# A decoder layer with a top-2 mixture of experts: routing on the unnormalized rows, whole-row gathers, a column-halved output product, slots dealt over the partitions

## What is computed

```python
y = jnp.concatenate([rmsnorm(yi, og[i]) for i, yi in enumerate((y_pool, y_rg, y_nsa, y_sc))], axis=-1)
x = x + jnp.einsum('blm,md->bld', y, lw['w_out'])
x = x + moe_ffn(rmsnorm(x, lw['norm_ffn_g']), lw['router_group_w'], lw['router_group_b'],
                lw['router_expert_w'], lw['router_expert_b'], lw['exp_w_gu'], lw['exp_w_down'])

def moe_ffn(x, wg_r, bg_r, we_r, be_r, w_gu, w_down):   # xt: the 520 rows
    lg = xt @ wg_r + bg_r                        # 4 groups, the best one is taken
    pg = softmax(lg);  gsel = argmax(lg)
    le = (xt @ we_r + be_r).reshape(T, 4, 8)     # 8 experts in each group
    tv, ti = top_k(le[gsel], 2)
    gate = pg[gsel] * softmax(tv)
    # for each of a token's two experts e:  a, b = split(x @ w_gu[e]);  y += gate * ((silu(a) * b) @ w_down[e])
```

## Time and profile before

| what | value |
|---|---|
| time, median of 3 runs (lowest, highest) | 896.74 us (896.69, 897.82) |
| the profiled execution's own time | 897.07 us |
| its span, first to last instruction | 895.3 us |
| granted TensorE clock, mean over the span | 0.962 of full speed |
| PE busy | 745.3 us (83%) |
| DVE, ACT, POOL busy | 217.6, 137.9, 186.9 us (24%, 15%, 21%) |
| moved by the DMA engines | 247.55 MB, 276 GB/s over the span |
| chain that ended last, by engine | PE 39%, SP's queue 33%, DVE 11%, DMA 11% |

### The profile page before, as it was taken

One profiled execution on the slowest core, in us unless ns is written; L12 is line 12 of the kernel. 1 busy time (PEld: TensorE's weight loads), 2 busy tenths in 40 slices (PEclk: granted clock), 3 DMA queues, 4 the chain that ended last, 5 costly groups with the idle time before them and its releaser, 6 DMA issues.

```text
span 895.3 us, 10055 instructions
## 1 busy us (share of the span) xinstructions
PE 745.3 (83%) x3636; PEld 384.8 (43%) x3636; DVE 217.6 (24%) x546; ACT 137.9 (15%) x338; POOL 186.9 (21%) x186
## 2 busy tenths in 40 slices
PE   3999999979898999829999997777777777787783
PEld 3788688857666545613333332222222222222220
DVE  4331104267759322171011110010010010100110
ACT  4212313013253401100000000000000000000000
POOL 6010000150300000011322331322312313223121
PEclk9999999989897999859999999999999999999997
DMA  9642823010510294458999999999999999999981
GB/s 309 127 135 60 262 103 102 4 69 1 207 77 1 83 423 181 164 225 339 413 410 408 408 406 415 415 408 417 409 412 414 410 413 416 408 416 409 413 341 30
DMA packets 75812, 247.55 MB, mean 276 GB/s; under 512 B 24796, under 2 KB 44139, under 8 KB 51163
## 3 DMA queue, kind: packets, MB, share of 16 engines
q1 hardware_dynamic: 62625, 232.00, 65.5%
q0 software_dynamic: 11776, 8.58, 4.4%
q10 hardware_dynamic: 1378, 6.54, 1.8%
HBM read 240.99 MB, written 24.92 MB: 297 GB/s over the span
## 4 chain that ended last, share of the span: by engine, by line
PE 39%; SPq 33%; DVE 11%; DMA 11%; issue 3%; ACT 2%; POOL 0%; ACTq 0%; DVEq 0%; POOLq 0%
PE bank L1063 36%; SPq L570 23%; SPq L577 9%; DMA reg_b<-in_exp_w_gu 6%; PE bank L1066 3%; DMA reg_a<-in_exp_w_gu 3%; DMA reg_x<-in_x_prompt 1%; DVE reg_a L1722 1%; DVE reg_a L1802 1%; DVE reg_y L1973 1%; DVE reg_a L1712 1%; DVE reg_x L1712 0%; DVE small L1763 0%; POOL small L673 0%; DVE reg_a L1714 0%
## 5 line engine op out<-in xcount | busy, mean ns | idle before, releaser
L1063 PE MATMUL bank<-reg_w,reg_y 128*64 128x512 f32 (+2 forms) x512 | 136.9, 585 | 19.3 <-DMA reg_w<-in_exp_w_gu 19.3
L1063 PE MATMUL bank<-reg_b,reg_y 128*64 128x512 f32 x528 | 124.3, 601 | 25.8 <-DMA reg_b<-in_exp_w_gu 18.0
L1063 PE MATMUL bank<-reg_a,reg_y 128*64 128x512 f32 x528 | 124.5, 607 | 24.0 <-DMA reg_a<-in_exp_w_gu 17.8
L1977 DVE TENSOR_TENSOR reg_y<-reg_y,bank 128x256 f32<-128x256 f32 x32 | 13.5, 421 | 426.5 <-ACT reg_y L1046 426.5
L1063 PEld LDWEIGHTS bank<-reg_w,reg_y 128*64 128x64 f32 (+2 forms) x512 | 46.1, 146 | 104.5 <-issue 59.6
L1063 PE MATMUL bank<-reg_b,reg_w 128*128 128x260 f32 x384 | 85.3, 383 | 0.0
L1063 PEld LDWEIGHTS bank<-reg_b,reg_y 128*64 128x64 f32 x528 | 34.1, 136 | 106.8 <-issue 56.5
L1063 PEld LDWEIGHTS bank<-reg_a,reg_y 128*64 128x64 f32 x528 | 34.5, 138 | 105.3 <-issue 50.6
L1063 PEld LDWEIGHTS bank<-reg_b,reg_w 128*128 128x128 f32 x384 | 72.7, 190 | 12.0 <-issue 1.1
L673 POOL TENSOR_TENSOR small<-small 128x1 f32<-128x1 f32 (+4 forms) x18 | 20.2, 1125 | 198.1 <-DVE small L1855 68.1
L739 POOL DMA_INDIRECT out_y_p<-reg_y,reg_q x16 | 25.3, 1581 | 170.6 <-ACT reg_y L1050 170.6
(11 more groups left out here) (341 smaller groups left out, 656.9 us busy)
## 6 DMA issues: line engine op xcount, KB each, us to landing
reg_a<-in_exp_w_gu SPq DMA_DIRECT2D x44, 1024.0 KB, 28.1
reg_b<-in_exp_w_gu SPq DMA_DIRECT2D x44, 1024.0 KB, 28.3
reg_w<-in_exp_w_gu SPq DMA_DIRECT2D x40, 1024.0 KB, 28.2
reg_a<-in_exp_w_down SPq DMA_DIRECT2D x22, 1024.0 KB, 28.5
reg_b<-in_exp_w_down SPq DMA_DIRECT2D x22, 1024.0 KB, 28.6
reg_h<-in_exp_w_down SPq DMA_DIRECT2D x20, 1024.0 KB, 28.8
reg_w<-in_w_in SPq DMA_DIRECT2D x9, 1024.0 KB, 10.7
reg_w<-in_w_out SPq DMA_DIRECT2D x1, 4096.0 KB, 13.2
```

The source lines that it names most:

```text
L1063: return eng.matmul(out, lhsT, rhs, start=start, stop=stop, skip_group_check=True)
L1977: tt(hid[b], silu[b], bank[2 + b][:, 256:512], ALU.mult).then_inc(S["hid_made"], 1)
```

## The change

Four things are changed together.

1. **The router reads the raw residual.** The gain is multiplied into the router's weights once (POOL, `rtw_scaled`), and the root is applied to the router's result, one number per token (`group_choice`). `second_norm` and the reordered `h2` are gone: PE turns `x1` itself (`turn_x1`).
2. **Whole raw rows are gathered.** `ffn_in` now holds `x1`. A gather takes 64 partitions of 4 KB. PE turns them with 8 transposes of 64 partitions at a column stride of 8, `copy_xe` multiplies by the gain, the root goes through its own three bf16 pieces to the slots (`gate_table` has 192 columns) and is applied in the silu's scale; the gate of a slot carries the other root.
3. **The output product goes by column halves.** PE makes the left halves of all tiles, then the right halves, with transposes and routing matmuls between their chunks. DVE chooses experts in two groups: tiles 4, 0, 1 early, tiles 2, 3 late. SP issues expert 2's down parts after the last transposes of the mixers, and its gate and up parts after Y3.0 and Y3.1.
4. **Slots are dealt over the partitions.** `cap_iota` gives slot 4a+b the rank a+16b, where it gave slot s the rank s.

The diff, cut:

```diff
-            eng.iota(cap_iota, pattern=[[0, 2], [1, CAP]], base=0, ...)
+            eng.iota(cap_iota, pattern=[[0, 2], [1, 16], [16, 4]], base=0, ...)
...
+            eng.tensor_tensor(rt_w, rt_w, params[:, P_FFN_G:P_FFN_G + 8].unsqueeze(2).to_broadcast([128, KC, 36]), ALU.mult).then_inc(S["rtw_scaled"], 1)
...
             def gather(e):
-                idx = bass.IndirectOffsetOnAxis(ap=row_of[:, e:e + 1], axis=0)
-                eng.indirect_dma_start(xe_rows[e % 2], None, h2_halves, idx, bounds_check=2 * T - 1, oob_is_err=False).then_inc(x_gathered[e % 2], 16)
+                at = slice(CAP * (e % 2), CAP * (e % 2) + CAP)
+                idx = bass.IndirectOffsetOnAxis(ap=row_of[0:CAP, e:e + 1], axis=0)
+                eng.indirect_dma_start(xe_rows[at], None, x1_dram, idx, bounds_check=T - 1, oob_is_err=False).then_inc(x_gathered[e % 2], 16)
...
# PE
-            for n in range(NTILE):
-                project_out(n)
-                if n:
-                    turn_h2(n - 1)
-            route(3)
-            turn_h2(4)
-            route(4)
+            for n in range(1, NTILE):
+                drained(eng, f"NT{TILES[n]}")
+                project_out(n, 0, {6: (turn_x1, (0, 0)), 7: (turn_x1, (0, 1))} if n == 1 else {3: (route, (0,))} if n == 2 else {})
+            project_out(1, 1, {4: (turn_x1, (1, 0))})
+            for n in range(2, NTILE):
+                project_out(n, 1, {2: (turn_x1, (n - 1, 1)), 5: (route, (n - 1,)), 7: (turn_x1, (n, 0))})
...
+            eng.wait_ge(S["mask_made"], 1)
+            positions("posA", range(3))
+            turn_x1(4, 1)
+            route(4)
+            eng.wait_ge(S["mask_made"], 2)
+            positions("posB", [3, 4])
...
-                    ins = mm(bank[0][:, 64:160], in_slot[:, m_, :], ids[:, m_ // 5, m_ % 5, 2:5]..., m_ == 0, m_ == 9)
+                    ins = mm(bank[0][:, 64:256], in_slot[:, m_ // 2, m_ % 2, :], scale_ids[:, m_ // 2, m_ % 2]..., m_ == 0, m_ == 9)
...
-                for j in range(4):
-                    ins = turn(bank[1][:, 128 * j:128 * j + 128], xe_rows[b][:, 128 * j:128 * j + 128])
+                by_channel = xe_rows[at, :].rearrange("n (p c) -> n c p", c=KC)
+                for c in range(KC):
+                    ins = eng.transpose(bank[1][:, CAP * c:CAP * c + CAP], by_channel[:, c, :], ident[at, at])
...
# DVE
-                second_norm(n)
+            drained(eng, "Y4.0")
+            tt(x1[0:NS, 4, :], x1[0:NS, 4, :], y_smp, ALU.add).then_inc(S["x1_smp"], 1)
+            ask_rstd(0)
+            for n in range(1, NTILE):
+                add_half(n, 0)
+            for n in range(1, 3):
+                add_half(n, 1)
+                ask_rstd(n)
+            early, late = range(3), range(3, 5)
+            group_choice(early)
+            add_half(3, 1)
+            expert_choice(early)
+            ask_rstd(3)
+            add_half(4, 1)
+            count_before(early, "posA")
+            ask_rstd(4)
+            find_slots(pk, early)
+            group_choice(late)
+            expert_choice(late)
+            count_before(late, "posB")
...
+            link(tt(gate, gate, rstd[:, 0:5].unsqueeze(2).to_broadcast([128, 5, 2]), ALU.mult))
+            for which in range(2):
                 for k in range(2):
-                    ins = eng.tensor_copy(ids[:, k, :, 2 + piece], ohp[:, k])
+                    factor = gate[:, :, k] if which == 0 else rstd[:, 0:5]
+                    ins = tt(ohp[:, :, k, :], oh[:, :, k, :], factor.unsqueeze(2).to_broadcast([128, 5, N_EXP]), ALU.mult)
+                link(ins)
+                for piece in range(3):
+                    out = scale_ids[:, :, :, 3 * which + piece, :]
+                    ins = eng.tensor_copy(out, ohp)
...
+                    if piece < 2:
+                        link(tt(ohp, ohp, out, ALU.subtract))
...
-                eng.tensor_copy(xe[b], bank[1][:, :].rearrange("p (j s n) -> p j s n", j=4, s=2)).then_inc(S["xe_made"], 1)
+                tt(xe[b], bank[1][:, :].rearrange("p (c n) -> p c n", c=KC), gain_x.unsqueeze(2).to_broadcast([128, KC, CAP]), ALU.mult).then_inc(S["xe_made"], 1)
...
# SP
-            eng.wait_ge(bank_full[bank_of["Y3.1"]], turn_of["Y3.1"] + 1)
-            load_gu(2, 2)
-            eng.wait_ge(S["h2_stored"], 16 * NTILE)
-            eng.wait_ge(bank_full[bank_of["hTb3"]], turn_of["hTb3"] + 1)
-            load_down(2, 2)
+            eng.wait_ge(bank_full[bank_of["NT3"]], turn_of["NT3"] + 1)
+            load_down(2, 2)
+            eng.wait_ge(bank_full[bank_of["Y3.0"]], turn_of["Y3.0"] + 1)
+            load_gu(2, 2, parts=(0, 1))
+            eng.wait_ge(bank_full[bank_of["Y3.1"]], turn_of["Y3.1"] + 1)
+            load_gu(2, 2, parts=(2, 3))
```

More of the change, by code:

```diff
@@ L153, in psum_jobs @@
         take(f"NT{i}")
-    last = None
     take("L", 7)
-    for i in TILES:
-        take(f"Y{i}.0")
-        if i < 4:
-            take(f"Y{i}.1")
-        if last is not None:
-            take(f"hTa{last}")
-            take(f"hTb{last}")
-        last = i
-    take("hTa3")
-    take("hTb3")
-    take("pos")
+    first, *others = TILES
+    take(f"Y{first}.0")
+    take(f"Y{others[0]}.0")
+    take(f"hTa{first}")
+    take(f"hTb{first}")
+    for i in others[1:]:
+        take(f"Y{i}.0")
+    take(f"Y{others[0]}.1")
+    take(f"hTa{others[0]}")
+    for last, i in zip(others, others[1:]):
+        take(f"Y{i}.1")
+        take(f"hTb{last}")
+        take(f"hTa{i}")
+    take("posA")
+    take(f"hTb{others[-1]}")
+    take("posB")
     take("cnt", 6)
@@ L351, in layer_kernel @@
         thr = small.cut(8)
-        valid = small.cut(5)
+        valid = small.cut(1)
         minus_half = small.cut(160)
@@ L561, in _, with load_gu @@
             eng.dma_start(x1[:, 0:4, :], x_dram).then_inc(S["x_reloaded"], 16)
-            def load_gu(e, g, free=None):
+            def load_gu(e, g, free=None, parts=range(GU_PARTS)):
                 width = KC // GU_PARTS
-                for part in range(GU_PARTS):
+                for part in parts:
                     lo = part * width
@@ L994, in _, with square, x1_turned @@
             eng.dma_start(o["rgh_s"].rearrange("l b c -> (l b) c"), tail_rows[16:24, 768:1024]).then_inc(S["tails_stored"], 16)
-            def sums(n):
+            def square(n, half):
                 i = TILES[n]
                 r = ROWS[i]
-                if i < 4:
-                    drained(eng, f"Y{i}.1")
-                else:
-                    ps = taken(eng, "Y4.0")
-                    for w in range(4):
-                        ins = copy(y_smp[:, 256 * w:256 * w + 256], ps[32 * w:32 * w + NS, 0:256])
-                    copied(ins, "Y4.0")
-                    eng.wait_ge(S["x1_smp"], 1)
-                eng.activation(h2[0:r, i, :], x1[0:r, i, :], ACT.Square, accum_out=sumsq[0:r, i:i + 1]).then_inc(S["x1_ss"], 1)
-            def h2_turned(n):
+                at = slice(512 * half, 512 * half + 512)
+                earlier = 5 + n if half and n else n + (n > 0) + half
+                if earlier >= 2:
+                    eng.wait_ge(S["x1_ss"], earlier - 1)
+                scratch = squares[0:r, 512 * (earlier % 2):512 * (earlier % 2) + 512]
+                eng.activation(scratch, x1[0:r, i, at], ACT.Square, scale=1.0 / 32, accum_out=x1_sq[0:r, n, half:half + 1]).then_inc(S["x1_ss"], 1)
+            def x1_turned(n, k):
                 i = TILES[n]
@@ L1907, in _, with add_half @@
[L1907 to L1913 removed]
+            def add_half(n, half):
+                i = TILES[n]
+                at = slice(512 * half, 512 * half + 512)
+                ps = taken(eng, f"Y{i}.{half}")
+                copied(tt(x1[:, i, at], x1[:, i, at], ps[:, :], ALU.add), f"Y{i}.{half}")
@@ new lines, in count_before, with find_slots @@
+            def count_before(g, job):
+                at = slice(g[0], g[-1] + 1)
+                ps = taken(eng, job)
+                cols = ps[:, 32 * g[0]:32 * g[-1] + 32].rearrange("p (t e) -> p t e", t=len(g))
+                for k in range(2):
+                    ins = tt(ohp[:, at, k, :], oh[:, at, k, :], cols, ALU.mult)
+                copied(ins, job)
+                drained(eng, job)
+                link(eng.tensor_reduce(pk[:, at, :], ohp[:, at], X_AXIS, ALU.add))
+            def find_slots(at, g):
+                lo, m_ = g[0], len(g)
+                tt(in_slot[:, lo:lo + m_].rearrange("p t k s -> p (t k) s"), cap_iota.unsqueeze(1).to_broadcast([128, 2 * m_, 2 * CAP]),
+                   at[:, lo:lo + m_].rearrange("p t k -> p (t k)").unsqueeze(2).to_broadcast([128, 2 * m_, 2 * CAP]), ALU.is_equal).then_inc(S["in_slot_made"], 1)
```

398 lines of the change are left out of this document (199 added, 199 removed).

## The result

The changed kernel takes **908.67 us** (median of 4 runs, 907.26 to 909.59) against 897.28 us before (4 runs, 896.69 to 897.98): ratio 1.0125, 95% interval 1.0106 to 1.0144. It is 11.4 us slower, where 884.6 us and a gain were predicted. The profiled execution took 909.55 us, its span is 907.7 us.

What follows compares the result with a forecast made beforehand. From expert 3 on only the weight transfers were taken to set the pace. Start -5.4 and finish -6.7 us summed to -12.1 on the profiled 897.07, giving 885.0, or 884.6 at the median; range 880.5 to 892.5.

Steps and rivals of the forecast that it cites:

- The bytes don't change: a row of 4 KB is gathered once where two halves were: Gathers beside the expert weights: same bytes in whole rows, only where the rows sit changes; no cost to the stream counted.
- The middle of the experts still at 1.02 and 410 GB/s: Sign that the forecast is right: mid-expert DMA share and rate stay as in the kernel before.
- Bound by the stream from expert 3 on: Experts from about 400 us: only weight transfers set the pace; PE is busy 82 of 100 us.
- Start, 5.4 us: Chain before the first freed-buffer weight issue: SP issues at 399.5 instead of 404.94, bounds 3 to 8 us.
- DVE's late choice: Expert choice after the last tile's routing: DVE starts at 377.8, 3.7 us sooner; mask at 381.35.
- pieces: bf16 splitting of gate and root on DVE after the indices: 7.3 us instead of 4.8, done at 393.7.
- The new last wait: Before expert 0, which begins at 395.7 against 401.13: the bf16 splitting is waited for last, no longer the gather.
- Finish, 6.7 us: End of the stream: dealt slots cut the slowest engine's 9.7 us excess to 3; bounds nothing and 9.7.
- Rival B: Start works, finish doesn't: gathers over 64 partitions lie on eight engines; 891 to 893 us; 16%.
- Rival C: Finish works, but bf16 splitting takes 3.9 us twice, start gains 3.4 or less; 887 to 889 us; 6%.
- Rival D: Slower: occupied slots fall on half of the engines for everything, excess 35.7 instead of 9.7; 917 us; 4%.
- Rival E: Early choice blocks DVE, a bank is late, PE stalls in the projection, no finish gain; 895 to 897 us; 4%.

Runs made afterwards that it cites:

- the half-row run: Changed kernel with half rows gathered over 128 partitions again, 4 transposes and a fitting weight channel order, slots still dealt: 884.27 us, ratio 0.9858.
- 64 of 128 filled: Changed kernel with each whole-row gather spanning 128 partitions, only 64 with an index in bounds, one buffer instead of two: 885.04 us, ratio 0.9858.
- the deal alone: Kernel before with only the slot order changed, slot 4a+b taking rank a+16b: 889.46 us against 897.47, ratio 0.9914.

## Why the prediction was wrong

**The step that failed** is the sentence "The bytes don't change: a row of 4 KB is gathered once where two halves were", with which the narrower gather was priced at nothing on the stream. The bytes didn't change (8.58 MB in both). But every us of the stream is one of the end, as the prediction itself had said, and the gathers over 64 partitions beside it cost every engine 17.5 us. The trace of before had no such transfer, and the step should have had bounds: the missing row was a reason for a price on both sides, not for none. "The middle of the experts still at 1.02 and 410 GB/s" was named as the sign; 1.02 came true and 410 didn't. The same narrower gather also took the finish: of the 24.1 us between 884.6 and 908.67, 17.5 are the slower stream, and 6.3 are the finish, where 0.4 of the 6.7 us came.

Point by point:

- *Bound by the stream from expert 3 on:* right. PE's extra 0.4 us an expert (1.09 for the 8 transposes, 0.66 for the 4 of before, 0.75 in the half-row run) cost nothing with 64 of 128 filled: 885.04 against 884.27, intervals 0.9839 to 0.9877 and 0.9837 to 0.9879.
- *Start, 5.4 us:* right, 5.1 in the profile, and 889.46 - 884.27 = 5.2 between the deal alone and the half-row run. Of its steps, DVE's late choice began at 378.9 (377.8 predicted: the last half ended at 374.6 instead of 372.6, and the routing behind it took 1.95 us instead of 2.6), indices done at 387.4 (386.4), pieces at 394.4 (393.7), expert 0 at 396.1 (395.7), first refill at 399.9 (399.5). The new last wait is the pieces, as said. That the sum is so near is luck in part: the projection ended 2.0 us later than predicted, and the shorter routing and pieces took most of it back.
- *Finish, 6.7 us:* right wherever the gather spans 128 partitions: 8.0 us in the deal alone (6.7 of them the spread), 5.7 in half rows, the spread down from 9.7 to about 3. In the change it gave nothing: 9.3.
- *Rival B* (a gather over 64 partitions on eight engines; finish falls in two halves): its sign came. The halves are in the rows, and as it said, the new unevenness is as large as the old one. It came by the deal, not by the 64 partitions alone: without the deal the first gather had up to 16 packets under way at once. Its price of 891 to 893 missed, because it too left the middle at 410.
- *Rival C* (the pieces eat the start): no, as the last piece at 394.4 and the first refill show.
- *Rival D* (slower, the occupied slots on half of the engines for everything) had the right sign with the wrong cause. Its reason against itself, that transfers dealt one by one would finish together before, is sound for the adds and for gathers over 128 partitions; the mistake was to take it for the transfers over 64 as well, which the kernel before didn't have. No share of 0.6 to 0.9 stood in the middle.
- *Rival E* (a bank late in the projection): no.

Without the failed step the sum was 884.6, and the two versions that keep the rest of the change and span 128 partitions measured 884.27 and 885.04.

## What to carry to other kernels

Where a stream of transfers over 128 partitions sets the pace, let a gather beside it span 128 partitions too, even if half of its indices are out of bounds; over 64 the whole stream slows. (Other kinds of transfer were not tried.) The indices out of bounds cost little: in the packet records each is a packet of 4 bytes and 9 ns, 2048 more of them here, 1.2 us for each engine over the whole kernel. Read GB/s beside the busy share when the bytes of a transfer are the same but its shape is not. And an operation whose shape no row shows gets a price on both sides, all the more where it runs beside the resource that sets the end.

## What was not expected of the hardware

- A gather over 64 partitions slows the weight transfers beside it from 410 GB/s to between 391 and 394 (500 to 600 us) at the same busy share of 1.02, whether it is asked as whole rows or as half rows, and though it moves 0.13 MB for 6 MB of weights. The loss is made while its packets are under way: near them the weights' packets take 388 ns instead of 310, away from them 314. A stretch in which one gather of the changed kernel passes (its packets start from 624.3 to 626.2), and one between two:

```profile
624.60:626.60 2.00, 1.59 (x8) 0.29 (x4) 0.00 (x0) 0.00 (x0) 0.00 (x0) 1.00 1.01 320
632.00:635.00 3.00, 2.44 (x12) 0.70 (x14) 0.00 (x0) 0.00 (x0) 2.39 (x3) 1.00 1.04 434
```

- Which engines a gather over 64 partitions uses depends on which slots are filled, by another rule than over 128: 27 neighbouring slots have up to 16 packets under way at once, 27 slots with a number modulo 4 of 0 or 1 at most 10. With the transfer over 128 partitions and the same 64 in bounds, the latter have at most 9, and cost nothing.
- The column stride of a transpose matters more than its shape. At full clock, turning 64 rows of 1024 float32 values takes 0.66 us as 4 transposes of 128x128 with contiguous columns and 0.75 at a stride of 4; 0.71 us as 8 of 64x64 with contiguous columns (whole-row gathers on the kernel before) and 1.09 at a stride of 8 (the change); and 4.02 us as 16 float32 matmul passes against 64 columns of the identity, at the stride of 8.
